# Two projections ahead of a gated attention: one stage of strip pairs, norm factors put into the weights, residual stored by another queue

## What is computed

```python
def rms_norm(x, g, eps=RMS_EPS):
    xf = x.astype(jnp.float32)
    y = xf * lax.rsqrt(jnp.mean(xf * xf, axis=-1, keepdims=True) + eps)
    return (y * g.astype(jnp.float32)).astype(x.dtype)

def shared_kv(h, kv_norm_g, w_kv, b_f, k_gain):
    kvf = rms_norm(h, kv_norm_g) @ w_kv
    k = rms_norm(split_heads(kvf[..., :D_MAIN], N_MAIN_HEADS), k_gain)
    v = split_heads(kvf[..., D_MAIN:2 * D_MAIN], N_MAIN_HEADS)
    log_f = jax.nn.log_sigmoid((kvf[..., 2 * D_MAIN:] + b_f).astype(jnp.float32))
    c = jnp.cumsum(log_f, axis=1)
    return k, v, c

# layer 1
u = rms_norm(x, mix_norm[l]) @ b_w_in[j]
q = rms_norm(split_heads(u[..., :D_MAIN], N_MAIN_HEADS), b_q_gain[j])
o = forgetting_attention(q, k_sh, v_sh, c_sh).reshape(bsz, t, D_MAIN)
main = o * jax.nn.sigmoid(u[..., D_MAIN:2 * D_MAIN])
x = merge_and_ffn(x, l, main, u[..., 2 * D_MAIN:])
```

## Time and profile before

| | us |
|---|---|
| median of three runs | 3123.95 (3118.14 to 3124.06) |
| the profiled execution | 3127.95, its span 3126.1 |
| last matmul of feed-forward 0 | 1690.75 |
| first and last matmul of `kv` | 1695.83, 1860.7 |
| `kv`'s matmuls at the lower clock level | 1695.83 to 1700.1 |
| first and last matmul of `in_b` | 1877.10, 2052.2 |
| first load of the gated attention | 2057.81 |
| its first matmul | 2064.93 |

### The profile page before, as it was taken

One profiled execution on the slowest core, in us unless ns is written; L12 is line 12 of the kernel. 1 busy time (PEld: TensorE's weight loads), 2 busy tenths in 40 slices (PEclk: granted clock), 3 DMA queues, 4 the chain that ended last, 5 costly groups with the idle time before them and its releaser, 6 DMA issues. The chain is left out here.

```text
span 3126.1 us, 54820 instructions
## 1 busy us (share of the span) xinstructions
PE 2868.7 (92%) x23385; PEld 2307.1 (74%) x23385; DVE 1490.7 (48%) x2032; ACT 933.5 (30%) x1522; POOL 1113.1 (36%) x1050
## 2 busy tenths in 40 slices
PE   7999588888769999999999989978979899999998
PEld 6888367777647788888887767745648788888887
DVE  6233255666442844445224636637742755555222
ACT  3111233333242533333002113125541533333100
POOL 6353033332212544444434223211103444444432
PEclk9999699999889999999999999989999999999999
DMA  6332200000033132225323222232204132224421
GB/s 203 97 112 68 94 17 23 23 23 11 3 95 124 52 116 85 81 81 173 99 67 109 76 83 68 81 122 82 82 21 142 54 108 81 81 81 145 137 70 67
DMA packets 261082, 261.17 MB, mean 84 GB/s; under 512 B 9254, under 2 KB 221340, under 8 KB 259560
## 3 DMA queue, kind: packets, MB, share of 16 engines
q1 hardware_dynamic: 255480, 240.22, 24.0%
...
q0 software_dynamic: 480, 0.03, 0.0%
...
## 5 line engine op out<-in xcount | busy, mean ns | idle before, releaser
L276 POOL TENSOR_TENSOR w_lo_b<-w_raw_b,w_hi_b 128x512 fp32r<-128x512 f32 (+1 forms) x474 | 609.4, 1287 | 380.8 <-ACT w_hi_b L308 363.0
L358 PE MATMUL ps<-b_hi,w_hi_b 128*128 128x512 f32 x1176 | 458.1, 390 | 4.3 <-ACT x_res L2152 4.3
L358 PE MATMUL ps<-b_lo,w_hi_b 128*128 128x512 f32 x1176 | 457.6, 389 | 0.0
L358 PE MATMUL ps<-b_hi,w_lo_b 128*128 128x512 f32 x1176 | 457.6, 389 | 0.0
L272 POOL CAST w_hi_b<-w_raw_b 128x384 fp32r<-128x384 f32 (+1 forms) x222 | 128.4, 578 | 773.4 <-PE ps L330 552.0
L358 PEld LDWEIGHTS ps<-b_hi,w_hi_b 128*128 128x128 f32 x1176 | 220.7, 188 | 52.2 <-ACT x_res L2152 6.0
L358 PEld LDWEIGHTS ps<-b_hi,w_lo_b 128*128 128x128 f32 x1176 | 220.7, 188 | 45.9
L358 PEld LDWEIGHTS ps<-b_lo,w_hi_b 128*128 128x128 f32 x1176 | 220.8, 188 | 45.6
L330 PE MATMUL ps<-b_hi,w_hi_b 128*128 128x512 f32 x768 | 238.8, 392 | 15.9 <-DVE b_lo L2263 15.6
L2316 DVE TENSOR_TENSOR x_res<-x_res,ps 128x1024 f32<-128x1024 f32 x64 | 78.1, 1221 | 341.4 <-PE ps L330 331.3
L330 PE MATMUL ps<-b_hi,w_lo_b 128*128 128x512 f32 x768 | 237.4, 390 | 0.0
...
## 6 DMA issues: line engine op xcount, KB each, us to landing
w_raw_b<-in_w_gate_up SPq DMA_DIRECT2D x88, 512.0 KB, 4.2
act_dram<-x_res SPq DMA_DIRECT2D x44, 512.0 KB, 6.0
stage<-act_dram ACTq DMA_DIRECT2D x32, 512.0 KB, 3.4
...
w_raw_a<-in_a_w_in SPq DMA_DIRECT2D x23, 512.0 KB, 4.6
u_dram<-evac_a SPq DMA_DIRECT2D x23, 512.0 KB, 3.0
...
```

The source lines that it names most:

```text
L276: nc.gpsimd.tensor_tensor(self.wlo[:, r, 0:n, :], source, self.whi[:, r, 0:n, :].bitcast(F32), ALU.subtract).then_inc(self.w_lo, 1)
L358: mm = self.nc.tensor.matmul(self.ps[:, bank, :], w[:, r, k, :], h[:, block, k, :], start=(start and k == 0 and a == 0 and h is self.bh), ...
```

## The change

The two stages become one (`phase_project`). The forget gates' strip is plain and comes first; the other 26 strips form 13 pairs, `PROJ_PAIRS`, by the feed-forward's scheme: six of (keys, values), one of two heads, four of (head, gate), then one of two memory heads and one of two gates. Since both norms share the sum of squares, `x` is split and summed once, without a factor, and each weight strip is multiplied by its norm's factors on GpSimd, in place in the raw buffer (`gain_strip`), two strips per pair, ahead of the split of blocks 4 and 6 of the pair before. Vector scales each result by the token's norm, which is kept in `rms` in SBUF.

The work on `x` moves in part to the last group of feed-forward 0: as each tile is done, ScalarE stores it to `x_dram` (`keep`), forms its `hi` and squares it; Vector forms its `lo`, adds the squares and, once a tile's store has landed, begins the four sums of `x` in place (`next_sums`). The eighth tile's part, and the splits of the four sums, stand at the start of the new stage. Units of that group run in the order 0 to 7 where they ran 4 to 7 and 0 to 3 (also in layer 1, for all groups but the first).

A pair `p` on TensorE is: product 0, the head sum of pair p - 1, products 1 to 3, the second head sum or the turn of values of pair p - 1, products 4 to 6. `before` is the heads of pair p - 1.

```diff
+PROJ_PAIRS = ([(("keys", c), ("vt", PAIRS + c)) for c in range(PAIRS)] + [(("head", 0), ("head", 1))]
+              + [(("head", 2 + i), ("gate", PAIRS + i)) for i in range(4)] + [(("head", 12), ("head", 13)), (("gate", 10), ("gate", 11))])
...
+    def gain_strip(self, pool, s):
+        _, tiles, cols, _ = self.strips[s]
+        pool.wait_ge(self.w_raw[s % RAW], 16 * (s // RAW + 1))
+        w = self.raw[:, s % RAW, 0:tiles, 0:cols]
+        at = self.place_params[self.gains[s]]
+        by = self.params[:, at:at + tiles].rearrange("p (k a) -> p k a", a=1).broadcast_to([P, tiles, cols])
+        self.nc.gpsimd.tensor_tensor(w, w, by, ALU.mult).then_inc(self.w_gain, 1)
...
+            @block.sync
...
+                at = 0
+                for p in range(1, N + 1):
+                    while at < len(loads) and loads[at] <= self.units[u0 + p + 2].strips[-1]:
+                        self.load_strip(sp, loads[at])
+                        at += 1
...
+                    if p > 1:
+                        for i in (1, 0) if pairs[p - 1][1][0] != "head" else (0, 1):
+                            store(p - 1, i)
+                for i in range(2):
+                    store(N, i)
+                for s in loads[at:]:
+                    self.load_strip(sp, s)
...
+            @block.gpsimd
+            def _(pool):
+                for j in range(split_from, split_to):
+                    for p in range(1, N):
+                        if j in (first(p) + 4, first(p) + 6):
+                            self.gain_strip(pool, self.units[u0 + p + 1].strips[(j - first(p)) // 6])
+                    self.split_block(pool, j)
...
+            @block.scalar
...
+                cast_sum(3)
+                self.cast_block(act, first(1) + 6)
+                act.wait_ge(rms_spread, 1)
+                act.wait_ge(t_lo, 4)
+                copy(rms, ps[:, 6:8, :]).then_inc(rms_kept, 1)
...
+                    act.wait_ge(self.block_done, j + 1)
...
+                    snap(p, 0, 0, b)
+                    ahead(0)
+                    if before:
+                        root_head(before[0])
+                    if len(before) == 2:
+                        square_head(before[1])
+                    ahead(1)
...
+                for i in range(2):
+                    open_gate(N, i)
...
+            @block.vector
...
+                for p in range(1, N + 1):
+                    j, b = first(p), base(p)
+                    before = heads_of(p - 1)
+                    if p > 1:
+                        scale(p - 1, 1)
+                    if p < N:
+                        self.early_sums(dve, u0 + p + 1)
+                    if before:
+                        finish_head(before[0])
+                    dve.wait_ge(self.block_done, j + 2)
+                    dve.wait_ge(snapped, 4 * p - 3)
+                    tt(out(p, 0)[:, 0, :], out(p, 0)[:, 0, :], ps[:, b + 2, :], ALU.add).then_inc(summed, 1)
+                    if p < N:
+                        self.late_sums(dve, u0 + p + 1)
+                    dve.wait_ge(self.block_done, j + 5)
+                    dve.wait_ge(snapped, 4 * p - 1)
+                    tt(out(p, 1)[:, 1, :], out(p, 1)[:, 1, :], ps[:, b, :], ALU.add).then_inc(summed, 1)
+                    if len(before) == 2:
+                        finish_head(before[1])
...
+                    dve.wait_ge(self.block_done, j + 6)
+                    tt(out(p, 0)[:, 1, :], out(p, 0)[:, 1, :], ps[:, b + 1, :], ALU.add).then_inc(summed, 1)
+                    scale(p, 0)
+                scale(N, 1)
...
+            @block.tensor
...
+                    self.product(pe, j, b, 0, True, False)
+                    if before:
+                        head_sum(before[0])
+                    self.product(pe, j + 1, b + 2, 1, True, True)
+                    pe.wait_ge(t_lo, 2)
+                    pe.wait_ge(snapped, 4 * p - 3)
+                    self.product(pe, j + 2, b, 2, False, False)
...
+                    pe.wait_ge(t_lo, 4)
+                    pe.wait_ge(summed, 3 * p - 1)
+                    self.product(pe, j + 6, b, 6, False, True)
...
+                def keep(k):
+                    act.wait_ge(self.psum_free, KT * (G - 1) + k + 1)
+                    act.dma_start(self.x_dram[:, k, :], X[:, k, :]).then_inc(kept[k] if k < KT - 2 else self.x_last[k - KT + 2], 16)
```

476 lines of the change are left out of this document (377 added, 99 removed).

## The result

The changed kernel takes 3099.2 us (median, 3095.3 to 3104.2), the kernel before 3124.0 in the same measurement: a ratio of 0.9926, 95% interval 0.9907 to 0.9944. Predicted were 3101, that is 22.7 us less; the medians lie 24.8 us apart.

What follows compares the result with a forecast made beforehand. TensorE, 92% busy, was taken as the bound. Start 42.7, twelve pairs with head sums and turns 267.5, waits 8.7 and 6.0, end 17.5, queue 2 make 344.4 us against 367.06, hence 3101 us, range 3083 to 3119.

Steps and rivals of the forecast that it cites:

- lag of the last group: End of feed-forward 0's last group: added Vector work on x makes the last two tiles overrun, 1.2 us (0 to 3).
- wait at product 2: First pair: TensorE waits 3.5 us for ScalarE's copy of product 0, which stands behind `t_lo` 4.
- 14 head sums: In the pairs on TensorE: each head sum adds 2.45 us, as in the strips before; 34.3 us in all.
- waits before product 6: GpSimd's multiplication holds Vector's fourth sum of weights: 1.5 us in pairs 9 to 11, 0.7 in 2 to 7; 8.7 us.
- pair 9 behind two heads: TensorE waits 4.5 us for a square behind two Vector reciprocals, plus 1.5 us lower clock: 6.0 us.
- pair 4 behind the forget gates: Pair 4, after the forget gates' operations on Vector: the prediction had no term for a delay here, 0 us.
- end: Last matmul to barrier: late third-strip load of output weights and GpSimd's remainders of it take 17.5 us, against 5.6.
- queue ahead of the attention: After the barrier: four loads stand ahead of the attention's on the queue, 2 us more (0 to 4).
- No blocks: Rival, chance 0.20: GpSimd's operations do not hold Vector's; no waits at product 6, 5.0 us less at start; 3087 us.
- cheap end: Rival, chance 0.10: the stage's last load and its remainders hide behind the stores' landing; 6 us less, 3095 us.
- Late store: Rival, chance 0.08: last group's tile stores land after 6 us, not 2.6; lag grows by up to 10; 3111 us.
- GpSimd paces: Rival, chance 0.14: slower GpSimd multiplications (g us each) delay fourth sum and last remainder; at g = 4, 3136 us.

Runs made afterwards that it cites:

- gain26: Changed kernel with the first GpSimd norm-factor multiplication of each pair moved ahead of the split of block 2: stage 326.4 us against 339.3, whole 3086.0 us.
- onegain: Changed kernel with both strips of a pair multiplied in one GpSimd operation of 128x2048: stage 358.3 us against 339.3, whole 3116.4 us.
- fgate: Changed kernel with the running sum of the forget gates and its store one pair later: stage 336.1 us against 339.3, whole 3096.7 us.
- nogain: Changed kernel with GpSimd's norm-factor multiplications cut from 128x1024 to 128x32, result wrong: stage 326.5 us against 339.3, whole 3082.6 us.
- loads: Changed kernel with all five remaining loads of output weights issued ahead of the last two stores: stage 341.3 us against 339.3, whole 3097.9 us.
- loads2: Changed kernel with four of the five remaining output-weight loads ahead of the last two stores, the fifth behind: stage 338.8 us against 339.3, whole 3096.3 us.
- gain2: Changed kernel with each norm-factor multiplication done twice, result's scale wrong: stage 375.0 us against 339.3, whole 3135.2 us.

## Why the prediction was right, point by point

The total was right within 2 us, on terms of which several were off and made up for each other. That closeness is in part luck: the stage gave 27.8 us where the sum forecast 22.7, and the medians lie 3 us nearer together than the stages do. In us, from the last matmul of feed-forward 0:

| step | predicted | measured |
|---|---|---|
| lag of the last group | 1.2 | 0 |
| barrier | 2.1 | 2.3 |
| forget strip, token sums, lower clock | 13.6 | 14.9 |
| spread, products 0 and 1 | 7.2 | 7.5 |
| wait at product 2 | 3.5 | 4.1 |
| lower clock and five products | 15.1 | 15.3 |
| twelve pairs at 19.04 | 228.5 | 228.5 |
| 14 head sums | 34.3 | 25 |
| six turns | 4.7 | 5.4 |
| waits before product 6 | 8.7 | 5.5 |
| pair 9 behind two heads | 6.0 | 7.0 |
| pair 4 behind the forget gates | 0 | 5.2 |
| end | 17.5 | 18.2 |
| queue ahead of the attention | 2 | 0 |
| sum | 344.4 | 338.9 (the stage: 339.3) |

How the measured terms of the pairs are read: in gain26, where no product 6 waits, a (head, gate) pair takes 20.85 us, that is 19.04 and 1.8 for the head sum, and a (keys, values) pair 21.75, that is 0.9 more for the turn. In the changed kernel the two pairs from the head sum at 1761.68 to that at 1810.40 take 48.7, which is 5.2 over twice 21.75. From the second head sum of pair 8 (1887.10) to that of pair 10 (1928.57) are 41.5, where 12.7 and 20.85 would do, and 0.9 of the difference is a wait before product 6.

**Head sums.** The largest miss, 9 us. The step took 2.45 us from the strips of before, with an idle 0.48 ahead of each. After, that idle time is gone (1950.50 above), and where nothing waits a (head, gate) pair takes 20.85 us, 1.8 over the 19.04 of a pair without a head sum. Why the 0.48 went no run tells.

**Waits before product 6.** The mechanism was right: the fourth sum was held (2.38), and product 6 waited in six pairs (nine were forecast; pairs 3, 4 and 6 had no wait). The size was off because a free multiplication takes 1.9 us and the prediction took 2.4, from the mask addition. With the 0.5 us less, 1.0 of the forecast 1.5 us would be left in a (head, gate) pair, and 0.84 was measured. The mean of the multiplications in the pairs, 2465 ns, lies in the forecast 2.3 to 2.5 only because Vector holds many of them; three of the stage took over 3.3 us (3.88 and, at the start, twice 3.94), which the prediction had named as a sign of being wrong. Each such wait cost 0.25 more than it shows (21.93 for a pair against 20.85). What the prediction did not see is that the holds cost in more places than this: without the multiplications the stage is 12.8 us shorter, not 5.5. They also drew out the chains on Vector that end in the waits of pairs 4 and 9. "No blocks", a rival at 3087, came within 1 us of gain26 (3086.0), where the fourth sum is not held, but by luck: it added 5.0 us at the start, of which gain26 shows nothing in the wait at product 2 (4.08, as before the move), and left out the 6.3 in pairs 4 and 9.

The page "SBUF — State Buffer" of the Trainium skill ("Who interferes with whom") says that the two engines' shared port pair is an exclusive lock, and that a Vector instruction with at most one SBUF input, outside the modes that use both pairs, does not contend. onegain (4.10 us behind 4.05) agrees with the first and gain26 (6.54 us around two operations) with the second. The page "GPSIMD Engine Reference" ("4.1 Engine selection") of the Trainium skill speaks against giving GpSimd a two-input product. No run here has the multiplications on Vector, so whether the advice would have paid is open; on GpSimd they cost 13 us of the path in their first place and nothing measurable in their second.

**Pair 4.** A term that the prediction had put at nothing: it counted Vector's chain in a steady pair only, and the forget gates' two operations (5.0 us) stand in pair 3, ahead of the scaling of the head. fgate shows it: 3.2 us by moving one of them. By nogain the holds have as large a part in it: without them 4.4 of the 5.2 us are gone with the two operations in place.

**Pair 9, the start, the end.** As predicted, in place and in size: the wait of 4.14 for the square behind two reciprocals, 4.08 at product 2 behind `t_lo` 4, and GpSimd's remainders of a late load ahead of the barrier. In the changed kernel the late load set the end, as the step had it. But when loads go ahead of the stores, the stores land late and set it instead (loads, loads2), so the cheap end, at 6 us less, came by neither order that was tried.

**Late store.** Did not come: the tiles' stores landed in 2.9 us beside the weights' loads by ScalarE's queue, in 3.0 by SyncE's.

**GpSimd paces.** The rival's total was near: for g = 4 it gave 3136, and gain2 with two times 1.9 measured 3135.2. Its way to it was not: by its rule 3.8 us give 3131, the two terms do not stand in one pair together, and 3.4 us of the loss lie at the start. It failed to come because g was 1.9.
